# Giving the first gates buffer a place of its own, and reading it back in three pieces

## The reference, cut to what matters

```python
q = (xf @ wq).reshape(n, PEER_HEADS, 2, PEER_HALF)
s = jnp.einsum('nhpd,hpkd->nhpk', q, subkeys)
...  # top 16 of each half, top 16 of their 256 sums: expert ids and best_s
gate = jax.nn.softmax(best_s, axis=-1)
h = jnp.einsum('nd,nhkd->nhk', xb, u[eb])
coef = gb * jax.nn.gelu(h, approximate=False)
return jnp.einsum('nhk,nhkd->nd', coef, v[eb])
```

## Time and the profile before

| | us |
|---|---|
| median of 3 runs | 2049.67 |
| lowest and highest | 2046.78 to 2054.2 |
| profiled execution | 2070.54 |
| its span | 2068.8 |
| PE busy | 1919.1 |
| DVE busy | 1532.9 |
| ACT busy | 764.1 |

### The profile page before, as it was taken

One profiled execution on the slowest core, in us unless ns is written; L12 is line 12 of the kernel. 1 busy time (PEld: TensorE's weight loads), 2 busy tenths in 40 slices (PEclk: granted clock), 3 DMA queues, 4 the chain that ended last, 5 costly groups with the idle time before them and its releaser, 6 DMA issues.

```text
span 2068.8 us, 34098 instructions
## 1 busy us (share of the span) xinstructions
PE 1919.1 (93%) x13250; PEld 1627.3 (79%) x13250; DVE 1532.9 (74%) x2826; ACT 764.1 (37%) x1113; POOL 609.5 (29%) x403
## 2 busy tenths in 40 slices
PE   5989998888999879999999999969999999999996
PEld 4978876348983349999999999957887877889995
DVE  6277994314446248999989999958787868879898
ACT  3222454442220033334346666533333333333332
POOL 2322343000000015555552222252222323235550
PEclk9988999787999989999999999989999999999998
DMA  3211232001005024434468988899999999999991
GB/s 125 72 62 41 92 112 72 0 1 43 3 4 203 0 85 152 137 131 140 147 240 295 319 313 322 306 380 356 345 369 354 348 319 351 356 317 339 377 356 68
DMA packets 173720, 416.53 MB, mean 201 GB/s; under 512 B 13953, under 2 KB 89217, under 8 KB 170385
## 3 DMA queue, kind: packets, MB, share of 16 engines
q1 hardware_dynamic: 119728, 256.16, 36.1%
q0 software_dynamic: 36864, 134.23, 17.2%
q10 hardware_dynamic: 16992, 24.26, 3.2%
HBM read 363.08 MB, written 51.51 MB: 200 GB/s over the span
## 4 chain that ended last, share of the span: by engine, by line
PE 40%; DVE 14%; DMA 6%; issue 1%; ACT 0%; SPq 0%; DVEq 0%; ACTq 0%
PE ps L2012 21%; PE ps L1927 11%; PE ps L1931 5%; DMA gates<-dense_gates 3%; PE ps L1985 3%; DVE is_place L2099 2%; DMA coef<-parked_gelu 2%; DVE is_place L2094 1%; DMA w_staged<-in_stream 1%; DVE picks L2102 1%; DVE top_at L2060 1%; DVE top_at L2069 1%; DVE s_head L2063 1%; DVE best_at L2060 1%; DVE best_at L2069 1%
## 5 line engine op out<-in xcount | busy, mean ns | idle before, releaser
L2012 PE MATMUL ps<-w_hl,coef_hl 128*128 128x512 f32 x2304 | 539.7, 395 | 23.5 <-DVE coef_hl L2186 23.5
L2012 PEld LDWEIGHTS ps<-w_hl,coef_hl 128*128 128x128 f32 x2304 | 436.8, 190 | 119.6 <-DVE coef_hl L2186 25.6
L1927 PE MATMUL ps<-h_hl,w_hl 128*128 128x384 f32 (+1 forms) x2304 | 447.8, 346 | 15.6 <-DVE h_hl L2032 8.7
L1927 PEld LDWEIGHTS ps<-h_hl,w_hl 128*128 128x128 f32 x2304 | 406.9, 190 | 30.2 <-issue 9.1
L1542 POOL DMA_INDIRECT gathered_rows<-in_u_rows,pick_index x128 | 161.6, 1262 | 379.1 <-DVE pick_hidden L1552 359.4
L1861 ACT ACTIVATE w_hl<-w_staged 128x1024 fp32r<-128x1024 f32 x143 | 152.2, 1064 | 246.7 <-PE ps L2012 153.5
L1542 POOL DMA_INDIRECT gathered_rows<-in_v,pick_index x128 | 168.5, 1316 | 239.9 <-DVE h_tok L1561 201.6
L1931 PE MATMUL ps<-h_hl,w_hl 128*128 128x384 f32 (+1 forms) x1152 | 230.0, 340 | 0.0
L1931 PEld LDWEIGHTS ps<-h_hl,w_hl 128*128 128x128 f32 x1152 | 203.3, 188 | 5.0
L1801 POOL TENSOR_TENSOR w_hl<-w_staged,w_hl 128x1024 fp32r<-128x1024 f32 x64 | 164.4, 2571 | 136.4 <-ACT w_hl L1826 111.9
L1561 DVE SCALAR_TENSOR_TENSOR h_tok<-gathered_rows,pick_hidden,h_tok 128x1024 f32<-128x1024 f32 x128 | 164.1, 1282 | 6.7 <-DVE h_tok L1561 0.5
(11 more groups left out here) (315 smaller groups left out, 2558.0 us busy)
## 6 DMA issues: line engine op xcount, KB each, us to landing
w_staged<-in_stream SPq DMA_DIRECT2D x132, 512.0 KB
h1T<-in_v SPq DMA_DIRECT2D x66, 512.0 KB
w_staged<-in_v SPq DMA_DIRECT2D x62, 512.0 KB
dense_gates<-lot SPq DMA_DIRECT2D x24, 1024.0 KB
gates<-dense_gates SPq DMA_DIRECT2D x16, 1536.0 KB
w_staged<-in_w_in_t SPq DMA_DIRECT2D x40, 512.0 KB
parked_gelu<-h1T ACTq DMA_DIRECT2D x102, 192.0 KB
coef<-parked_gelu SPq DMA_DIRECT2D x102, 192.0 KB
```

What stands on the lines that cost most here:

```text
L1927: nc.tensor.matmul(ps[:, bank, 0:width], w_hl[:, j % RING, 0, P * k:P * (k + 1)], h_hl[:, part, k, lo:SEQ], start=(k == 0 and part == 0), ...
L2012: last = nc.tensor.matmul(ps[:, 2 + 2 * t + half, :], coef_hl[:, k % HLS, c, P * t:P * (t + 1)], w_hl[:, s % RING, v, 512 * half:512 * (ha ...
```

## The change

The first of the two gates buffers becomes a tile of its own, `gates0`, that shares no bytes with `lot`; room for it comes from seven small top-k tiles, which now lie in the part of SBUF that is free again after the top-k. The read of the first gates is cut into three DMAs: lots 0 to 15 are read behind the store of lot 17, lots 16 to 21 behind the store of lot 23, and lots 22 and 23 where the whole read was. Each waits for the stores of the lots that it reads. DVE waits for three increments where it waited for one.

```diff
+    FIRST_GATES = {LOTS - 7: slice(0, LOTS - 8), LOTS - 1: slice(LOTS - 8, LOTS - 2)}
+    FIRST_READS = len(FIRST_GATES) + 1
...
+        gates0 = sb("gates0", [P, LOTS, LOOP * LOT])
         with ExitStack() as first:
...
+            top = sb("top", [P, 2, NT, K], at=first)
...
         with ExitStack() as third:
-            gates = sb("gates", [P, 2, LOTS, LOOP * LOT], at=third)
+            gates1 = sb("gates1", [P, LOTS, LOOP * LOT], at=third)
+            gates = [gates0[:, :, :], gates1[:, :, :]]
...
+            def load_first_gates(lots):
+
+                for j in range(2):
+                    sp.wait_ge(lot_stored[j], 16 * (lots.stop // 2))
+                sp.dma_start(gates[0][:, lots], dense[lots, :, 0:LOOP * LOT].rearrange("l p k -> p l k")
+                             ).then_inc(gates_landed[0], 16)
...
                 sp.dma_start(dense[n], lot[:, n % 2, :, :].rearrange("p k n -> p (k n)")).then_inc(lot_stored[n % 2], 16)
+                if n in FIRST_GATES:
+                    load_first_gates(FIRST_GATES[n])
             load_from(FIRST_BEHIND + RING, QUERIES + PARKED)
-            for j in range(2):
-                sp.wait_ge(lot_stored[j], 16 * (LOTS // 2))
-            load_gates(0)
+            load_first_gates(slice(LOTS - 2, LOTS))
...
                 if k % LOOP == 0:
-                    dve.wait_ge(gates_landed[k // LOOP % 2], 16 * (k // LOOP // 2 + 1))
+                    reads = k // LOOP // 2 + (FIRST_READS if k // LOOP % 2 == 0 else 1)
+                    dve.wait_ge(gates_landed[k // LOOP % 2], 16 * reads)
```

More of the change, by code:

```diff
@@ L1656, in peer @@
         stage = [staged[:, j, :] for j in range(RING)] + [free[:, 1024 * j:1024 * (j + 1)] for j in (1, 3, 0, 2)]
[L1658 to L1664, removed]
         picks = sb("picks", [P, 3, NT, NP])
@@ L1678, in peer @@
             cand = sb("cand", [P, NT, K * K], at=first)
+            top = sb("top", [P, 2, NT, K], at=first)
+            top_at = sb("top_at", [P, 2, NT, K], U32, at=first)
+            keys = sb("keys", [P, 2, NT, K], at=first)
+            best = sb("best6", [P, NT, K], at=first)
+            best_at = sb("best_at", [P, NT, K], U32, at=first)
+            split_at = sb("split_at", [P, 2, NT, K], U32, at=first)
+            place = sb("place", [P, 2, NT, K], at=first)
             is_place = sb("is_place", [P, 2, NT, K, K], at=first)
@@ L1739, in load_gates @@
                     sp.wait_ge(weighed, LOOP * (i - 1))
-                sp.dma_start(gates[:, i % 2], dense[:, :, LOOP * LOT * i:LOOP * LOT * (i + 1)].rearrange("l p k -> p l k")
+                sp.dma_start(gates[i % 2], dense[:, :, LOOP * LOT * i:LOOP * LOT * (i + 1)].rearrange("l p k -> p l k")
                              ).then_inc(gates_landed[i % 2], 16)
+            def load_first_gates(lots):
[3 more added lines that the diff above has]
+                             ).then_inc(gates_landed[0], 16)
             def load_parked(k):
@@ L2181, in weigh @@
                 at = LOT * (k % LOOP)
-                v_.tensor_tensor(x, x, gates[:, k // LOOP % 2, :, at:at + LOT], ALU.mult).then_inc(weighed, 1)
+                v_.tensor_tensor(x, x, gates[k // LOOP % 2][:, :, at:at + LOT], ALU.mult).then_inc(weighed, 1)
             def low_coef(k):
```

## The result

The changed kernel is slower, by some 0.4%. Seven runs beside seven of the kernel before have the medians 2061.66 and 2050.3 us. The two medians alone stand 1.0055 apart; the ratio on record is 1.0046, with a 95% interval of 1.0025 to 1.0068, and all ratios in this document are of that kind. Two more measurements of the same kernel gave 1.0041 (1.0025 to 1.0057) and 1.0040 (1.0021 to 1.0059). By these ratios 8 to 9 us are lost on the clock, that is in measured time, where I had forecast 7.8 won; 2061.66 lies outside my range of 2033 to 2052.

The account below looks back on a forecast made before the run. PE was taken to bound the kernel, except in its wait for the first gates at the first sum. Terms: 14.8 - 2.2 - 4.3 - 0.5 = 7.8 us gained, 2049.67 to 2041.9, rounded to 2042; range 2033 to 2052.

Parts of the forecast that it names:

- The bound: At the first sum: PE waits 14.55 us for the read of the first gates; 2.05 us would stay.
- The clock at the first sum: At the first sum: 3.2 us lost to a lower clock behind the long wait, 0.9 charged for the remaining gap.
- The first piece, its pace: Behind the store of lot 17: 16 lots at 0.40 us each make the tile loads 6.4 us late.
- The first piece, what is given back: In the lots behind it: each gives back about 1.05 us, 4.2 in all, so 2.2 us arrive.
- The second piece: Behind the store of lot 23: 6 lots ahead of two tile loads count fully, 4.3 us, between 2.4 and 6.6.
- Next in line: At the fourth sum: its tile of `v`, issued only when the last gelu is parked, comes 0.5 us late.
- The third piece and the free edits: Read of the last two lots, 0.8 to 2.2 us, moved SBUF tiles, extra issues, changed wait count: all cost nothing.
- B: Tile loads later than forecast, pieces at 0.66 and 1.1 us a lot: gain 1.3 to 5 us, chance 0.20.
- D: In the lots: first piece as slow as the old read, 1.1 us a lot: 7.9 us slower, 2058, chance 0.13.
- C: In the sums: transfers, not PE, set the pace, early starts wait later: gain about 3 us, 2047, chance 0.11.
- signs of being wrong: PE stalls between 1290 and 1340, tiles end after 1391, first coefficient late, or later gates waits grow by the gain.

Follow-up runs that it names:

- buffer_only: The changed kernel's new places in SBUF, but all 24 lots read by one DMA where the kernel before reads them; ratios 1.0008 and 0.9984.
- after_late_v3: The changed kernel, but ACT rounds the coefficients of steps 1 and 2, and DVE makes step 2's remainder, before the fourth tile of `v`; ratio 1.0033.
- first_piece_only: The changed kernel, but only lots 0 to 15 are read early and lots 16 to 23 together at the end; ratio 1.0007.

## Why the prediction was wrong, step by step

**The bound: right.** The first sum did wait for the read, and with the pieces that wait falls from 14.55 to 2.11, as I put it (2.05).

**The clock at the first sum: wrong in size, and its reason not borne out.** I put 3.2 us down to the long wait and expected 2.3 of them back. The first sum got 1.3 shorter, and buffer_only has the same 6.0 us behind a wait of 14.16. Its granted clock in the changed kernel was 0.57, not the full one that I had named.

**The first piece, its pace: right.** I had the loads late by 6.4 us, at 0.40 a lot. ACT waits 7.58 - 1.00 = 6.6 us longer, 0.41 a lot.

**The first piece, what is given back: wrong in size.** I let every lot give back 1.05 us, ACT's own waits for PE. From lot 18 to 21 the lateness of the store falls only from 5.84 to 4.18, some 0.55 a lot. ACT waits for a load in each of these lots again (2.91 us in the next, not 1). I read this so: the loads are issued later and need their time, and the loop from store to load to rounding to copy to store has less slack than ACT has. No run tests that reading. So 4.2 us arrive and not 2.2; the wait of 4.91 at the end of the lots and the lower clock behind it (5.46 us for 16 matmuls) come with it.

**The second piece: wrong in size.** 4.3 us forecast, with 6.6 as the far end. The tile comes 12.4 us later behind the store of lot 17, of which 4.75 stood already when its load was issued: 7.6 for 6 lots, 1.27 a lot, beyond even the far end. I had even measured that place at 1.1 and then took the middle, on the argument that gathers that go ahead would be out of the way later. No such relief shows. Alone the piece has a ratio of 1.0026.

The Trainium skill's rule of turns ("DMA: Bandwidth & Descriptors", section on queues and rings) had spoken for the far end; the 0.41 and the 1.27 us for lots of the same size agree with it in direction, though no run here varied the gathers alone. That a single 512-byte run has a turn of its own was my reading: in that section an engine drains a whole packet of one queue, typically 9 to 17 descriptors, before it turns to the next. And the fit of 2.0 us plus the bytes, which I had given for any DMA, is in its section a measurement of DMAs that GpSimd issues; SP issues the reads here.

**Next in line: wrong, and the failing step in kind.** "The fourth sum needs that tile" is true of PE and false of ACT. ACT's list has `high_of(V_AT[0] + 3)` ahead of `high_coef(1)`, so the second sum waits for the fourth tile. I charged 0.5. The trace shows 6.57 of wait and then a second sum that is 2.7 us longer, 9.2 together; after_late_v3 shows that the wait at the second sum is due to the order. The load can't come early, as it waits until the last gelu is parked (5.82 us from its issue at 1392.33), and takes 6.11 us itself. In the kernel before, ACT had 1.66 us of it left at 1398.05, inside the first sum: the rest lay under the wait for the gates. This alone parts the first sum from the gain: first_piece_only wins 8 us at the first sum, 1 to 3 at the second and none at the third against the kernel before.

**The third piece and the free edits: right.** The places cost nothing on the clock (buffer_only), and the first sum has no longer wait for the last two lots.

**Rivals.** B had the shape, late loads and no further harm, but at the bottom of its own bounds it still saw 1.3 us of gain; with 4.2 and 7.6 for the loads and 6.6 for the tile of `v` my sum is 14.8 - 4.2 - 7.6 - 6.6 = -3.6, near the -4.4 of the trace at the second sum. With 1.3 for the 2.3 of clock at the first sum, and with the 2.7 at the second, it is -7.3, near the -7.1 of the trace at the third. D's mechanism did not come: the first piece did not crawl. C's did not either: the later waits of PE sum to 6.0 us in the first trace of the changed kernel and did to 8.9 before (5.0 in the second trace before, so this sum varies by itself). Of the signs of being wrong that I named, one came: the last tile ends at 1391.77, later than 1391. The new stall of PE, from 1339.5 to 1344.4, touches the end of the stretch from 1290 to 1340, so that PE had no wait in the lots was wrong too. No sign stood for the second sum.

## What to carry to other kernels

A transfer that nobody waits for is paid by the one behind it in its queue, here with 6.5 us for ACT where the order of the two loads and the read alone decided: place an early read behind the loads that have a waiter, or cut it so small that each part is made up for before the next. When a long wait is removed, go through each engine's list in its order and ask what it would have met next, for an instruction that is needed late can stand ahead of one that is needed soon. Count a slow stretch behind a wait with the wait: here the sum behind the 6.57 us cost 2.7 us more. And don't take the idle time of one engine for the slack of a loop over several: here 0.55 us a lot came back where that engine's idle time promised 1.05.

## What the runs showed that I had not expected

The same short runs went at 0.41 us a lot in the lots and at 1.27 in the tiles behind, at a distance of 78 us in one execution. And the store of the first lot stands anywhere from 1076.09 to 1091.24 us over the traces of all kernels, while the 190.9 us from there to lot 17 are the same to 0.1. Of the 14.8 us between the two traces of the kernel before, 8.6 lie ahead of that store, and of the 11.9 between the first and the third of the changed kernel 10.6: in these pairs most of the difference lies ahead of the reads that the change moves.
